# Delta rule: the 32x32 diagonal cells of the triangular inverses move to VectorE in the mLSTM stage, and the chunks run interleaved

## The reference

```python
def step(state, inp):
    r_t, w_t, k_t, v_t, kk_t, a_t = inp
    sa = jnp.einsum("bhvk,bhk->bhv", state, -kk_t)
    state = (state * w_t[:, :, None, :] + sa[..., None] * (kk_t * a_t)[:, :, None, :]
             + v_t[..., None] * k_t[:, :, None, :])
    return state, jnp.einsum("bhvk,bhk->bhv", state, r_t)
```

## Time and profile before

| | us |
|---|---|
| median of 3 runs | 4837.08 (4833.65 to 4839.87) |
| the profiled execution | 4837.8 |
| its span in the trace | 4836.0 |
| PE, PEld, DVE, ACT, POOL busy in the span | 3753.8, 2884.9, 1730.6, 969.7, 830.3 |

### The profile page before, as it was taken

How to read it: one execution, slowest core, us unless ns; L and a number is a source line. 1 busy time by engine, 2 the same in 40 slices (tenths; PEclk the granted TensorE clock), 3 DMA queues, 4 the chain that set the end, 5 groups by cost and what they waited for, 6 DMA issues and landing times. The chain is left out here.

```text
span 4836.0 us, 46526 instructions
## 1 busy us (share of the span) xinstructions
PE 3753.8 (78%) x16645; PEld 2884.9 (60%) x16645; DVE 1730.6 (36%) x2919; ACT 969.7 (20%) x1511; POOL 830.3 (17%) x734
## 2 busy tenths in 40 slices
PE   6658886999669865257777657978889879799969
PEld 3546665888446553056776536856678634466647
DVE  0113323023325365734444351226600010477713
ACT  1122222110123211212222112332100100133310
POOL 1042221111010022033333213210111000000021
PEclk7679998999879855578888888989999989899979
DMA  6232224212144011000000134641221202555254
GB/s 184 83 100 76 63 76 127 78 65 77 41 85 87 22 49 54 26 3 3 3 3 3 35 96 148 189 141 71 83 87 72 105 0 78 109 121 121 55 166 148
DMA packets 288456, 378.95 MB, mean 78 GB/s; under 512 B 67264, under 2 KB 226688, under 8 KB 273552
## 3 DMA queue, kind: packets, MB, share of 16 engines
q1 hardware_dynamic: 272344, 373.80, 26.6%
q10 hardware_dynamic: 16016, 3.95, 0.5%
HBM read 244.26 MB, written 133.43 MB: 78 GB/s over the span
## 5 line engine op out<-in xcount | busy, mean ns | idle before, releaser
L504 PE MATMUL f_psum_out<-f_x_high,f_w_high 128*128 128x512 f32 x1440 | 570.2, 396 | 98.3 <-DVE f_x_low L482 53.4
L504 PE MATMUL f_psum_out<-f_x_low,f_w_high 128*128 128x512 f32 x1440 | 567.7, 394 | 0.0
L504 PE MATMUL f_psum_out<-f_x_high,f_w_low 128*128 128x512 f32 x1440 | 567.0, 394 | 0.0
L504 PEld LDWEIGHTS f_psum_out<-f_x_high,f_w_high 128*128 128x128 f32 x1440 | 275.2, 191 | 165.4 <-issue 92.3
L504 PEld LDWEIGHTS f_psum_out<-f_x_high,f_w_low 128*128 128x128 f32 x1440 | 274.7, 191 | 58.2
L504 PEld LDWEIGHTS f_psum_out<-f_x_low,f_w_high 128*128 128x128 f32 x1440 | 275.1, 191 | 57.0
L393 PE MATMUL p_psum_proj<-p_w_high,p_h_high 128*128 128x512 f32 x512 | 219.2, 428 | 68.7 <-issue 45.0
L1032 PE MATMUL nbr_psum_o<-nbr_probT,nbr_v 128*128 128x512 f32 (+3 forms) x576 | 238.8, 496 | 19.1 <-ACT nbr_probT L1056 19.1
L2857 PE MATMUL rwkv_psum_b<-rwkv_x,rwkv_lt 128*128 128x128 f32 x768 | 139.8, 315 | 138.1 <-DVEq L2964 128.5
L393 PE MATMUL p_psum_proj<-p_w_high,p_h_low 128*128 128x512 f32 x512 | 215.0, 420 | 0.0
L393 PE MATMUL p_psum_proj<-p_w_low,p_h_high 128*128 128x512 f32 x512 | 213.8, 418 | 0.0
(11 more groups left out here) (490 smaller groups left out, 7540.6 us busy)
## 6 DMA issues: line engine op xcount, KB each, us to landing
f_w<-in_w_fm SPq DMA_DIRECT2D x45, 512.0 KB, 5.3
ada_w<-in_w_ada SPq DMA_DIRECT2D x6, 2048.0 KB, 17.3
scratch_qkmT<-p_qkT_out SPq DMA_DIRECT2D x32, 384.0 KB, 3.3
scratch_z1T<-f_out SPq DMA_DIRECT2D x10, 1024.0 KB, 4.7
p_z<-scratch_z1T SPq DMA_DIRECT2D x16, 640.0 KB, 5.9
p_xt<-in_x SPq DMA_DIRECT2D x16, 512.0 KB, 4.8
p_staging<-in_w_tok SPq DMA_DIRECT2D x8, 1024.0 KB, 4.9
scratch_hT<-p_h_slot SPq DMA_DIRECT2D x16, 512.0 KB, 5.8
```

Of the source, the lines that this page charges most:

```text
L504: last = nc.tensor.matmul(self.p_out[b][:, at], self.w_parts[b][w_part][:, k, :], self.x_parts[x_part][:, k, at], start=(k == 0 and i == 0 ...
```

## The change

1. `rwkv` runs `rwkv_factors`, then `mlstm`, then `rwkv_chunks`, inside one more phase that holds `big`, `to_next` and the cells.
2. `rwkv_factors` also multiplies, per chunk and head, KK by B (32 matmuls of 128 columns per block of features), ScalarE copies the four 32x32 diagonal cells of each (`keep_cells`), and SP stores them in DRAM in four DMAs (1 MB in all, rows of 128 bytes).
3. `mlstm` loads the 256 cells, two to a partition, and VectorE inverts I + L of all of them at once by substitution, column by column: 31 columns of two instructions, three columns per chunk from chunk 3 on (two behind the arguments, one behind `h1`). SP stores the inverses, and after the last output reads them back in four DMAs. All engines' loops are unrolled.
4. `rwkv_chunks` starts from these inverses: VectorE transposes them once, GpSimd places them (`fill`), and two levels remain (32 to 64 and 64 to 128: `coupled5`, `inverse5`, `coupled6`, `inverse6`), each four 64-column matmuls. The lower matrix, the slots, the level masks and their copies are gone; the products read `big` directly. The chunks are unrolled and interleaved: iteration c does the state work of chunk c, the inverse of chunk c + 1 and the products and transposes of chunk c + 2, with three buffers for what lives across, three PSUM banks in turn for products and transposes, and two for the state. The other engines' lists follow the same order; `through_state`, `remove`, `next_state` and `outputs` are the old matmuls in four parts.

```diff
+CELL = 32
+CELLS = P // CELL
+N_CELLS = NT * GH * CELLS
+def cells_of(dram):
+    return dram.rearrange("(g b) (i j) -> b i g j", b=CELLS, j=CELL)
...
+FIRST_CELLS = 3
+class Cells:
+    def __init__(self, ph, nc, d):
+        self.nc, self.d = nc, d
+        self.diagonal = ph.sb("diagonal", [P, NT * GH, CELL])
+        self.stored, self.low_in, self.x_done, self.x_stored, self.x_in = (
+            ph.sem(n) for n in ("stored", "low_in", "x_done", "x_stored", "x_in"))
+    def place(self, ph):
+        self.low, self.x = (ph.sb(n, [P, N_CELLS // P, CELL, CELL]) for n in ("cells_low", "cells_x"))
+        self.less = ph.sb("cells_less", [P, N_CELLS // P, CELL * CELL // 4])
+    def load(self, sp):
+        sp.wait_ge(self.stored, 16 * CELLS)
+        sp.dma_start(self.low[:].rearrange("p a i j -> p (a i j)"), self.d["rwkv_L"].rearrange("(p a) e -> p (a e)", p=P))\
+            .then_inc(self.low_in, 16)
+    def start(self, dve):
+        self.nc.vector.memset(self.x[:], 0.0)
+        dve.drain()
+        self.nc.vector.memset(self.x[:].rearrange("p a i j -> p a (i j)")[:, :, ::CELL + 1], 1.0)
+    def eliminate(self, dve, first, n):
+        for j in range(max(first, 0), min(first + n, CELL - 1)):
+            if j == 0:
+                dve.wait_ge(self.low_in, 16)
+            shape = [P, N_CELLS // P, CELL - 1 - j, j + 1]
+            less = self.less[:, :, 0:(CELL - 1 - j) * (j + 1)].rearrange("p a (i k) -> p a i k", k=j + 1)
+            below = self.x[:, :, j + 1:, 0:j + 1]
+            dve.drain()
+            self.nc.vector.tensor_tensor(less, self.low[:, :, j + 1:, j:j + 1].to_broadcast(shape),
+                                         self.x[:, :, j:j + 1, 0:j + 1].to_broadcast(shape), ALU.mult)
+            dve.drain()
+            last = self.nc.vector.tensor_tensor(below, below, less, ALU.subtract)
+            if j == CELL - 2:
+                last.then_inc(self.x_done, 1)
+    def store(self, sp):
+        sp.wait_ge(self.x_done, 1)
+        sp.dma_start(self.d["rwkv_X"].rearrange("(p a) e -> p (a e)", p=P), self.x[:].rearrange("p a i j -> p (a i j)"))\
+            .then_inc(self.x_stored, 16)
+    def spread(self, sp):
+        sp.wait_ge(self.x_stored, 16)
+        for b in range(CELLS):
+            sp.dma_start(self.diagonal[b * CELL:(b + 1) * CELL], cells_of(self.d["rwkv_X"])[b]).then_inc(self.x_in, 16)
+        sp.wait_ge(self.x_in, 16 * CELLS)
...
+            cells.load(sp)
+            for c in range(NT - 2):
+                sp.wait_ge(pe_done, c + 1)
+                sp.wait_ge(o_used, c + 1)
+                load(c + 2, c % 2)
+                store(c)
+            cells.store(sp)
             store(NT - 2)
             store(NT - 1)
+            cells.spread(sp)
...
+                cells.eliminate(dve, 3 * (c - FIRST_CELLS), 2)
+                cells.eliminate(dve, 3 * (c - FIRST_CELLS) + 2, 1)
+            cells.start(dve)
...
             sp.wait_ge(v_in, 16 * NB)
+            sp.wait_ge(cells_kept, 2 * NB)
+            for b in range(CELLS):
+                sp.dma_start(cells_of(d["rwkv_L"])[b], diagonal[b * CELL:(b + 1) * CELL]).then_inc(cells_stored, 16)
...
+            pe.wait_ge(clamped, NB)
+            pe.wait_ge(a_done, NB)
+            for n in range(NB):
+                pe.wait_ge(block_done, n + 1)
+                if n:
+                    pe.wait_ge(cells_kept, 2 * n)
+                for c in range(NT):
+                    at = slice(c * P, (c + 1) * P)
+                    for half, out in enumerate((p_w, p_a)):
+                        rows = slice(half * HD, (half + 1) * HD)
+                        last = nc.tensor.matmul(out[:, at], big[rows, n, F_KK, at], big[rows, n, F_B, at], start=True, stop=True)
+                        if c == NT - 1:
+                            last.then_inc(cells_out, 1)
...
+            def keep_cells(n):
+                for half, src in enumerate((p_w, p_a)):
+                    act.wait_ge(cells_out, 2 * n + half + 1)
+                    for b in range(CELLS):
+                        at = slice(b * CELL, (b + 1) * CELL)
+                        dst = diagonal[at].rearrange("p (c h) j -> p c h j", h=GH)[:, :, 2 * n + half, :]
+                        nc.scalar.activation(dst, chunks(src[at])[:, :, at], ACT.Copy)
+                    act.drain().then_inc(cells_kept, 1)
...
+                    keep_cells(n - 1)
+            keep_cells(NB - 1)
...
-    LEVELS = 7
-    slots = [sb(f"slot{b}", [P, NB, NF, P]) for b in range(2)]
-    lt = sb("lt", [P, LEVELS, GH, P])
-    xl = sb("xl", [P, LEVELS - 1, 2, 2, P])
+    AHEAD = 3
+    pads = [sb(f"pad{b}", [P, GH, F_KK, P]) for b in range(2)]
+    prod = [sb(f"prod{b}", [P, GH, 4, P]) for b in range(AHEAD)]
+    x, xT = ([sb(f"{n}{b}", [P, GH, P]) for b in range(AHEAD)] for n in ("x", "xT"))
+    p_a = [ps(f"a{n}", [P, BANK]) for n in range(3)]
+    p_xl, p_x, p_u, p_s, p_y = (ps(n, [P, BANK]) for n in ("xl", "x", "u", "s", "y"))
...
+            def fill(c):
+                if c >= AHEAD:
+                    pool.wait_ge(removed_out, c - AHEAD + 1)
+                    nc.gpsimd.memset(xT[c % AHEAD][:], 0.0)
+                    pool.drain()
+                    nc.gpsimd.memset(x[c % AHEAD][cell(1), :, cell(0)], 0.0)
+                    pool.drain()
+                heads_of = slice(c * GH, (c + 1) * GH)
+                for i in range(CELLS - 1):
+                    nc.gpsimd.tensor_copy(x[c % AHEAD][cell(i), :, cell(i)], cells.diagonal[cell(i), heads_of, :])
+                for i in range(CELLS):
+                    nc.gpsimd.tensor_copy(xT[c % AHEAD][cell(i), :, cell(i)], cells_T[cell(i), heads_of, :])
+                pool.drain().then_inc(x_filled, 1)
...
+            for c in range(-2, NT):
+                now, near, far = c >= 0, 0 <= c + 1 < NT, c + 2 < NT
+                if now:
+                    through_state(c)
+                if far:
+                    products(c + 2, (0, 1))
+                if near:
+                    coupled5(c + 1)
+                if now:
+                    remove(c)
+                if far:
+                    products(c + 2, (2, 3))
+                if near:
+                    inverse5(c + 1)
+                if now:
+                    next_state(c)
+                if far:
+                    turn(c + 2)
+                if near:
+                    coupled6(c + 1)
+                if now:
+                    outputs(c)
+                if near:
+                    inverse6(c + 1)
...
+            nc.vector.transpose(cells_T[:].rearrange("p g j -> p (g j)"), cells.diagonal[:].rearrange("p g j -> p (g j)"))\
+                .then_inc(turned, 1)
+            for b in range(AHEAD):
+                nc.vector.memset(prod[b][:], 0.0)
+            for ap in (*pads, *state, xl5, xl6):
+                nc.vector.memset(ap[:], 0.0)
+            dve.drain().then_inc(zeroed, 1)
...
+            def grow5(c):
+                dve.wait_ge(x5_out, c + 1)
+                out = each_head(p_x[:, 0:GW])
+                nc.vector.tensor_copy(x[c % AHEAD][cell(1), :, cell(0)], out[cell(1), :, cell(0)])
+                for a in range(2):
+                    nc.vector.transpose(xT[c % AHEAD][cell(2 * a), :, cell(2 * a + 1)], out[cell(2 * a + 1), :, cell(a)])
+                dve.drain().then_inc(x5_ready, 1)
...
+            for c in range(-2, NT):
+                if c + 2 < NT:
+                    mask(c + 2, range(GH))
+                if 0 <= c + 1 < NT:
+                    grow5(c + 1)
+                if 0 <= c < NT - 1:
+                    scale_state(c)
+                if c >= 1:
                     norm(c - 1)
...
 def rwkv(nc, d, g):
-    with nc.sbuf_tensor("rwkv_big", [P, NB, NF, T], F32) as big, nc.sbuf_tensor("rwkv_to_next", [P, NB, NT], F32) as to_next:
-        rwkv_factors(nc, d, g, big, to_next)
-        rwkv_chunks(nc, d, g, big, to_next)
+    ph = Phase(nc, "cells")
+    big, to_next = ph.sb("big", [P, NB, NF, T]), ph.sb("to_next", [P, NB, NT])
+    cells = Cells(ph, nc, d)
+    rwkv_factors(nc, d, g, big, to_next, cells.diagonal, cells.stored)
+    mlstm(nc, d, g, cells)
+    rwkv_chunks(nc, d, g, big, to_next, cells)
+    ph.close()
```

More of the change, by code:

```diff
@@ L2276, in mlstm, with pairs @@
     LOADS = 4
-    def pairs(eng, chunk):
-        with eng.Fori(0, NT // 2) as j:
-            for b in range(2):
-                chunk(2 * j + b, b, j)
+    def pairs(chunk):
+        for c in range(NT):
+            chunk(c, c % 2, c // 2)
     with nc.Block() as block:
@@ L2775, in _, with pad @@
             act.wait_ge(zeroed, 1)
-            def fill(c, b):
-                act.wait_ge(slot_free, c + 1)
-                nc.scalar.activation(slots[b][:], chunk_of(c), ACT.Copy)
-                for first in range(2):
-                    at = slice(first * HD, (first + 1) * HD)
-                    nc.scalar.activation(pads[b][at, first::2], chunk_of(c)[at, :, 0:F_KK + 1], ACT.Copy)
-                act.drain().then_inc(slot_ready, 1)
```

(38 more changed lines are left out.)

418 lines of the change are left out of this document (190 added, 228 removed).

## The result

The changed kernel takes 4446.59 us (median of 4 runs, 4445.64 to 4451.36) against 4836.97 (median of 4) on the same chip: ratio 0.9195, 95% interval 0.9179 to 0.9211, so 390 us less. The forecast was 4500 us, 338 less. The profiled execution has a span of 4443.9 us.

What follows compares the result with a forecast made beforehand. The prediction took the chunk loop to be bound by the latency of a serial chain handed between engines. Its terms, -438 + 17.5 + 39 + 42 + 1.5 = -338 us against 4837.8, gave 4500 us, range 4445 to 4585.

Steps and rivals of the forecast that it cites:

- Term 1: Chunk loop (`rwkv_chunks`): TensorE becomes the bound at 14.5 us a chunk, 256 us against 694.4, -438 us.
- slack walk: Chunk loop, new order laid out from t = 0: operands ready before TensorE needs them, 1.4 to 3.8 us of slack.
- rival B: Chunk loop: hand-overs stall TensorE after all, 18 to 20 us a chunk, 63 us more, 4563; chance 0.15.
- Rival D: Chunk loop: clock stays at 1.2 GHz, 28 us a chunk, 200 us more, about 4700; chance 0.05.
- Term 2: Factor stage: 64 more matmul instructions per half, second half's exposed, 12 plus 5 for copies: +17.5 us, between 12 and 22.
- Term 3: Stage boundaries: cells leave and return in 128-byte pieces, 21 us for 8192 pieces: +39 us, from +19 to +81.
- Rival C: Trips of the cells to and from DRAM: short packets cost double, 42 us more, 4542; chance 0.15.
- Term 4: mLSTM stage: substitution on VectorE, 37 us, 12 hidden in gaps, 17 for contention with GpSimd: +42 us, from 25 to 60.
- Rival E: Substitution in mLSTM: VectorE walks its patterns far below an element a cycle, kernel slower than before; chance 0.02.
- Term 5: End of the added phase: one phase more to close, +1.5 us.

Runs made afterwards that it cites:

- The doubled trips: Changed kernel with the four stores of the cells and the four loads of the spread each made twice, one behind the other: 4467.85 us, ratio 0.9239.

## Why the prediction was right, and where it was off

**How near it was.** The measured 4446.6 us lies within the range, but 1.6 us from its lower end, and 53 below the 4500. The terms' errors all have one sign and add up to 47 us; the rest lies in the unchanged stages. Terms 1, 2 and 3 each came out below the bound that the prediction gave for it: 13.94 us a chunk for 14.2, +11.4 for +12, +11.5 for +19. The whole stayed inside because the low end had also counted 17 us for the substitution and 10 for the start of the chunks, and neither came. So the mechanism was right, and that the range held is in part luck.

**What bounds the loop.** The forecast's main claim held: once the six levels are gone and chunks overlap, TensorE is the bound, never stands, and is granted its full clock. It was that claim that made -438, and the loop gave -449.

**Term 1, 11 us too small.** 14.5 us a chunk was the sum of work (14.2) and 0.3 for small gaps; measured are 13.94 in the steady part and no gaps, 8 us over 14 chunks. The groups of 64-column instructions take 0.83 to 0.92 and not 0.93; the products of two heads, 1.78, were as forecast. Start (13.8 for 13, 29.5 for 30) and end (11.9 from the start of the last chunk's product with the state, for the 7 and 5.5) were nearly right; the parts given for the 13 (2.3, 8.3 and 1.3) add up to 11.9. The slack walk held: no wait within the loop. The step "20 from above, if each of six hand-overs stalls TensorE by about 1 us" was wrong in kind, for it left the clock as it was. In the run without interleaving the hand-overs cost 4 us a chunk and the lower clock that comes with them 8 to 9 more; a loop as in rival B ended at 4645, not at 4563. Rival D is out by the window at 1.00.

**Term 2, 6 us too large.** The step that failed is "64 instructions, of 128 columns, 0.22 each while cold": 5.2 us and not 12, since pairs run at once. Its own prices, 0.22 for the first 6 us and 0.11 from there on, also give 10 and not 12, and the clock rose after 2.7 us. The eight copies took 4.9 of the 5 forecast. The first block's cells were hidden, as forecast (155.05 to 156.3 us).

**Term 3, 28 us too large, half of the miss.** Two steps failed. The price of a piece, 2.6 ns from a stretch with a DMA share of 0.55, is 0.7 ns; I took it that the count sets the limit, because the share was so low. The doubled trips have shares of nine tenths: in the stretch I scaled from (the eight stores of the earlier trace rows), the DMA engines stood nearly half of the time, and such a stretch gives no price. Divided by its share of 0.55, its 98 GB/s would be 178, an estimate, and this is the rate of the 128-byte pieces: between these two sizes the bytes set the time and not the count. And "the stores go ahead of mLSTM's constants and first chunk on SP's queue": what lies on the path is the issue of four DMAs (4.2 us, of which 2.5 show: 6.5 us from the last copy to the next stage, 4.0 from fox to the next stage before), for nobody but the contiguous load of the cells waits for their landing; constants and first chunk took 6.9 us for 6.7. The spread stands bare, as forecast, at 10.5 us for 25.5. Rival C was its opposite and is out.

**Term 4, right, by its parts too.** Forecast 37 us without company, 17 for GpSimd's, 12 hidden: 42. Measured 33.1 and 62 drains of 0.08, 38; 49.4 - 33.1 = 16.3 for GpSimd's; 40.4 in all, so 14 were hidden, which is a remainder and wasn't measured by itself. Rival E is out: 512 elements in these patterns take 0.69 to 0.73 us, contiguous ones 0.69 (L2442). The prediction took the place of the columns as given and costed only the gaps there; the waits for num_ready and h_rstd, 2.06 and 1.47 us a chunk before the change too, would have told it that all of term 4 could be hidden.

**Term 5.** No extra closing time is seen: 4.7 us from the last y_out to the next stage, 5.2 before.

Left open: how the 253 us of the loop that come without interleaving divide between fewer levels, dropped products and copies, and unrolling.

## What to carry to other kernels

When several chunks can be in flight, interleave them on the engine that is to be the bound, and count the clock in the gain: here the interleaving was worth 196 us, of which only 65 are the gaps themselves. Work put into a serial engine's chain costs nothing if it stands just ahead of a wait that is longer than it, and with no large product of GpSimd beside it; two slots moved by a few lines took a price of 40 us to about 1. A price per packet must come from a stretch in which the DMA engines are full.

## What the runs showed that I had not expected

- 128-byte pieces, 8192 of them, go in about 6 us by four DMAs, written or read: 0.7 ns a piece, some 175 GB/s. The contiguous load of the same bytes reached 328 to 426.
- With gaps of 0.5 to 2.0 us, 16% of the time in all, TensorE was granted 0.66 where the same work without gaps had 1.00; the slower instructions cost twice what the gaps themselves did.
- Products with 64 rows that alternate between the two halves of the array run two at a time, 0.21 us a pair at 1.2 GHz, in this kernel without any line that asks for it.
- VectorE's subtraction of 494 elements took 1.65 us beside GpSimd's product and 0.67 alone.
